# A decoder layer on one core: x's second half turned by VectorE, memory loaded earlier, GpSimd's units moved

## What is computed

```
h   = x + 1/2 * SwiGLU_1(norm(x))                 # w_ffn1_in, w_ffn1_out; d_ff = 5632
z   = norm(h) @ W_mix_in                          # columns B, C, H, U, V of 1024 each
y_c = B * causal_dwconv3(C * H)
y_g = U * (tril(W_s[head]) @ norm(V) + b)         # 8 heads x 128
h   = h + concat(y_c, y_g) @ W_mix_out
h   = h + XAttn(norm(h), norm(mem))               # 4 heads, w_xq, w_xk, w_xv, w_xo
h   = h + 1/2 * SwiGLU_2(norm(h))
out = norm_final(h)
```

## Time and profile before

| | |
|---|---|
| median of 3 runs (lowest to highest) | 2136.78 us (2136.63 to 2137.07) |
| the profiled execution: its time, its span | 2138.68 us, 2136.9 us |
| busy in the span: PE, DVE, ACT, POOL | 99%, 68%, 45%, 4% |
| traffic | 409 MB read, 192 GB/s over the span |
| share of the chain that ended last: PE, DVE, DMA | 95%, 3%, 1% |

### The profile page before, as it was taken

How to read it: one execution, slowest core, us unless ns; L and a number is a source line. 1 busy time by engine, 2 the same in 40 slices (tenths; PEclk the granted TensorE clock), 3 DMA queues, 4 the chain that set the end, 5 groups by cost and what they waited for, 6 DMA issues and landing times.

```text
span 2136.9 us, 23530 instructions
## 1 busy us (share of the span) xinstructions
PE 2124.8 (99%) x9480; PEld 1763.7 (83%) x9480; DVE 1462.7 (68%) x1754; ACT 964.2 (45%) x1090; POOL 92.9 (4%) x43
## 2 busy tenths in 40 slices
PE   9999999999999999999999999999999999999998
PEld 7888888888888888888888888888888888888887
...
GB/s 266 192 193 197 190 195 196 190 195 197 192 192 195 191 195 194 192 222 188 192 194 195 171 172 172 173 210 195 191 195 193 192 195 192 193 195 194 192 195 149
DMA packets 159825, 412.65 MB, mean 193 GB/s; under 512 B 12652, under 2 KB 14308, under 8 KB 159332
## 3 DMA queue, kind: packets, MB, share of 16 engines
...
HBM read 409.01 MB, written 2.10 MB: 192 GB/s over the span
## 4 chain that ended last, share of the span: by engine, by line
PE 95%; DVE 3%; DMA 1%; ACT 0%; issue 0%; ACTq 0%; DVEq 0%
PE ps L1180 94%; PE ps L1207 1%; DVE ps L745 1%; DVE w_lo L685 1%; DMA mem_nat<-in_mem 0%; DVE ps L1062 0%; PE ps L1265 0%; PE ps L1343 0%; DMA rows<-in_g_ffn 0%; PE ps L1230 0%; DVE memT_nat L756 0%; PE ps L1259 0%; DVE xT_lo L701 0%; DVE stage L848 0%; DVE stage L964 0%
## 5 line engine op out<-in xcount | busy, mean ns | idle before, releaser
L685 DVE TENSOR_TENSOR w_lo<-raw,w_hi 128x1024 fp32r<-128x1024 f32 x732 | 911.5, 1254 | 561.3 <-ACT w_hi L365 554.5
L365 ACT ACTIVATE w_hi<-raw 128x1024 fp32r<-128x1024 f32 x767 | 805.8, 1061 | 968.9 <-PE ps L1180 954.0
L1180 PE MATMUL ps<-w_hi,xT_hi 128*128 128x512 f32 x1848 | 494.5, 389 | 1.0 <-ACT w_hi L365 1.0
L1180 PE MATMUL ps<-w_lo,xT_hi 128*128 128x512 f32 x1848 | 493.9, 389 | 0.0
L1180 PE MATMUL ps<-w_hi,xT_lo 128*128 128x512 f32 x1848 | 493.9, 389 | 0.0
L1180 PEld LDWEIGHTS ps<-w_hi,xT_hi 128*128 128x128 f32 x1848 | 346.6, 188 | 73.3 <-DVE xT_lo L693 1.4
L1180 PEld LDWEIGHTS ps<-w_hi,xT_lo 128*128 128x128 f32 x1848 | 346.9, 188 | 72.0
L1180 PEld LDWEIGHTS ps<-w_lo,xT_hi 128*128 128x128 f32 x1848 | 346.9, 188 | 71.9
L745 DVE STREAM_TRANSPOSE ps<-stage 32x256 f32<-32x256 f32 (+1 forms) x464 | 241.4, 520 | 8.5
L1180 PE MATMUL ps<-w_hi,hidT_lo 128*128 128x512 f32 x700 | 188.5, 389 | 0.0
L1180 PE MATMUL ps<-w_lo,hidT_hi 128*128 128x512 f32 x700 | 188.5, 389 | 0.0
...
## 6 DMA issues: line engine op xcount, KB each, us to landing
...
```

The lines of the kernel that those rows point to most:

```text
L365: nc.scalar.activation(w_hi[:, u % RING, :], raw[:, u % RAW, :], ACT.Copy).then_inc(hi_ready, 1)
L685: nc.vector.tensor_tensor(w_lo[:, u % RAW, :], raw[:, u % RAW, :], w_hi[:, u % RING, :].bitcast(F32), ALU.subtract).then_inc(lo_ready, 1)
L1180: ins = nc.tensor.matmul(bank(s, t * GW + b * BLK, BLK), xs[:, k, t * P:(t + 1) * P], ws_[:, (unit0 + k) % (RING if ws_ is w_hi else RAW), ...
```

## The change

It has five parts.

1. x comes in six parts: tile 0 alone, tile 1 alone, then 2 and 3, 4 to 7, 8 to 11, 12 to 15. TensorE turns one identity block instead of four ahead of tile 0, tile 1 after the first passes of unit 0, tiles 2 and 3 a pass earlier.
2. Tiles 8 to 11 are turned by VectorE too, with the low parts of units 4 to 7 between the quarters; tiles 12 to 15 have those of units 9 to 12 between theirs. GpSimd makes the low parts of units 3, 5, 7, 9, 11 and 13 of this group instead of 7, 9, 11 and 13; such units are skipped in VectorE's list.
3. Memory is loaded in four parts of 512 KB inside V's weight loads, and SyncE's wait is gone. All of its first half is turned in U, the second in mix_out0 and mix_out1. `wsT`, which lay where memory goes, moves into `scratch`.
4. GpSimd's units in mix_out0 are now 5, 7, 9, 11, 13, 15 (they were the odd ones from 1), in k1 and v0 5, 7, 8, 10, 12, 14 (they were the odd ones from 5).
5. The gain product of the third piece of the end goes from VectorE to GpSimd.

The core of the diff:

```diff
-X_PARTS = ((0, 2), (2, 4), (4, 8), (8, 12), (12, 16))
+X_PARTS = ((0, 1), (1, 2), (2, 4), (4, 8), (8, 12), (12, 16))
...
-    pool_units = [*range(UNIT0["ffn1_in0"] + 7, UNIT0["ffn1_in0"] + 15, 2),
-                  *range(UNIT0["mix_out0"] + 1, done("mix_out1"), 2), *range(UNIT0["q0"] + 5, UNIT0["q0"] + 13, 2),
-                  *range(UNIT0["k1"] + 5, done("k1"), 2), *range(UNIT0["v0"] + 5, done("v0"), 2)]
+    pool_units = [*range(UNIT0["ffn1_in0"] + 3, UNIT0["ffn1_in0"] + 15, 2), *range(UNIT0["mix_out0"] + 5, done("mix_out0"), 2),
+                  *range(UNIT0["mix_out1"] + 1, done("mix_out1"), 2), *range(UNIT0["q0"] + 5, UNIT0["q0"] + 13, 2),
+                  *(UNIT0[name] + k for name in ("k1", "v0") for k in (5, 7, 8, 10, 12, 14))]
...
@@ SyncE @@
-            for name, c in (("C", 1), ("H", 2), ("B", 0), ("V", 4), ("U", 3)):
+            for name, c in (("C", 1), ("H", 2), ("B", 0)):
                 load_units(cols_src(w_mix_in, c * GW), UNIT0[name], KD)
-
-            sp.wait_ge(gated, 4)
-            sp.dma_start(mem_nat[:, :, :], mem[0].rearrange("(t p) n -> p t n", p=P)).then_inc(mem_loaded, 16)
+            for n in range(4):
+                load_units(cols_src(w_mix_in, 4 * GW), UNIT0["V"], 4 * n + 4, 4 * n)
+                t, c = n % 2, n // 2
+                sp.dma_start(mem_nat[:, t, c * GW:(c + 1) * GW], mem[0, t * P:(t + 1) * P, c * GW:(c + 1) * GW]
+                             ).then_inc(mem_loaded, 16)
+            load_units(cols_src(w_mix_in, 3 * GW), UNIT0["U"], KD)
...
@@ ScalarE @@
+            act.wait_ge(turned, TURN["x0"] + 1)
             nc.scalar.activation(xT_hi[:, 1, :], bank(1, 7 * SEQ, SEQ), ACT.Copy, scale=col("g_ffn1", 1)).then_inc(hi_taken, 1)
-            hi_units(0, 1, 2)
+            hi_units(0, 1, 3)
             hi_scaled(xT_hi, 0, "g_ffn1", 1, "x0", 1, 2)
-            hi_units(0, 2, 3)
             hi_units(0, 3, 4)
             hi_scaled(xT_hi, 0, "g_ffn1", 1, "x0", 2, 4)
-            hi_units(0, 4, 6)
+            hi_units(0, 4, 8)
             hi_scaled(xT_hi, HALF, "g_ffn1", 1, "x1", 0, 2)
-            hi_units(0, 6, 9)
+            hi_units(0, 8, 9)
...
@@ VectorE @@
-            lo_units(0, 4, 6)
-            lo_scaled(xT_lo, xT_hi, HALF, "g_ffn1", 1, "x1", 0, 2)
-            lo_units(0, 6, 7)
-            dve.wait_ge(x_loaded[4], 16)
-            dve.wait_ge(turned, TURN["x1"] + 2)
-            for q in range(4):
-                turn_blocks(h[:, :, 12 * P:D], 1, 4, 4 * q, 4 * q + 4, 4)
-                lo_units(0, 7 + q, 8 + q)
-            lo_units(0, 11, 12)
+            for part, u in ((4, 4), (5, 9)):
+                dve.wait_ge(x_loaded[part], 16)
+                for q in range(4):
+                    turn_blocks(h[:, :, X_PARTS[part][0] * P:X_PARTS[part][1] * P], 1, 4, 4 * q, 4 * q + 4, 4 * (part - 4))
+                    lo_units(0, u + q, u + q + 1)
+                if part == 4:
+                    lo_scaled(xT_lo, xT_hi, HALF, "g_ffn1", 1, "x1", 0, 2)
+                    lo_units(0, 8, 9)
             lo_scaled(xT_lo, xT_hi, HALF, "g_ffn1", 1, "x1", 2, 4)
-            lo_units(0, 12, 13)
...
-            lo_units(u, 8, 15)
-            dve.wait_ge(mem_loaded, 16)
-            turn_mem(0, u, 15, 0, 1)
-            turn_sbuf(memT_nat[:, 0:HALF, :], mem_nat[:, :, 0:GW], mem_turned, 2, 4)
+            lo_units(u, 8, 9)
+            dve.wait_ge(mem_loaded, 16 * 4)
+            turn_mem(0, u, 9, 0, 7)
+            turn_sbuf(memT_nat[:, 0:HALF, :], mem_nat[:, :, 0:GW], mem_turned, 14, 16)
...
-                lo_units(u, 3, 5)
+                lo_units(u, 3, 4)
                 dve.wait_ge(staged, STAGED[name] + TOK)
                 for i in range(4):
                     turn_blocks(stage[:, :, :], SET[name], HALF, 4 * i, 4 * i + 4)
-                    lo_units(u, 5 + i, 6 + i)
+                    lo_units(u, 4 + i, 5 + i)
...
-                lo_units(u, 9, 13)
+                lo_units(u, 8, 13)
...
-            end_gain(2)
             end_rstd(1, 4, 2)
...
@@ TensorE @@
-            group("ffn1_in0", xT_hi, xT_lo, 4, 5)
-            pe.wait_ge(x_loaded[3], 16)
+            group("ffn1_in0", xT_hi, xT_lo, 4, 6)
             pe.wait_ge(taken, TAKEN["x0"] + 4)
-            turn(from_half(h, 1), 1, 4, 0)
-            group("ffn1_in0", xT_hi, xT_lo, 5, 8)
+            group("ffn1_in0", xT_hi, xT_lo, 6, 8)
             pe.wait_ge(taken, TAKEN["x1"] + 2)
             group("ffn1_in0", xT_hi, xT_lo, 8, 12)
             pe.wait_ge(taken, TAKEN["x1"] + 4)
```

More of the change, by code:

```diff
@@ L135, in build @@
     stage = put("stage", [P, TOK, GW], F32)
+    at_scratch = place["at"]
     scratch = put("scratch", [P, GW], F32)
+    wsT = put("wsT", [P, HEADS, P], F32, at=at_scratch)
     ident = put("ident", [P, P], F32)
@@ L168, in build @@
     v_buf = put("v_buf", [P, TOK, GW], F32, at=big + 56 * KB)
-    wsT = put("wsT", [P, HEADS, P], F32, at=big + 64 * KB)
     sg = put("sg", [P, TOK, GW], F32, at=big + 80 * KB)
@@ L217, in build @@
         first_half = sem("first_half")
+        tile_turned = sem("tile_turned")
         tile_hi = sem("tile_hi")
@@ L253, in build @@
         gained = sem("gained")
+        gained_pool = sem("gained_pool")
         out_ready = [sem(f"out_ready{c}") for c in range(2)]
@@ L347, in low_units @@
                                             ALU.subtract).then_inc(lo_pool, 1)
-            low_units(pool_units[:4])
+            low_units(pool_units[:6])
             pool.wait_ge(ws_loaded, 16)
@@ L352, in _ @@
                                pattern=[[0, HEADS], [-1, P]], channel_multiplier=1).then_inc(ws_masked, 1)
-            low_units(pool_units[4:])
+            low_units(pool_units[6:])
+            pool.wait_ge(staged, STAGED["ffn2_out1"] + 3)
+            nc.gpsimd.tensor_tensor(stage[:, 1, 0:BLK], h[:, 1, GW:GW + BLK], g_fin[:, GW:GW + BLK],
+                                    ALU.mult).then_inc(gained_pool, 1)
         @block.scalar
@@ L455, in _ @@
             act.wait_ge(cols_ready, 1)
-            act.wait_ge(turned, TURN["x0"] + 1)
+            act.wait_ge(tile_turned, 1)
             nc.scalar.activation(xT_hi[:, 0, :], bank(1, 0, SEQ), ACT.Copy, scale=col("g_ffn1", 0)).then_inc(tile_hi, 1)
@@ L662, in _ @@
             nc.scalar.activation(h[:, 1, BLK:GW], h[:, 1, BLK:GW], ACT.Copy, scale=rstd[:, 1:2]).then_inc(end_ready[1], 1)
-            act.wait_ge(gained, TOK + 3)
+            act.wait_ge(gained_pool, 1)
             nc.scalar.activation(h[:, 1, GW:GW + BLK], stage[:, 1, 0:BLK], ACT.Copy,
@@ L973, in _ @@
             lo_plain(yT_lo, yT_hi, HALF + 4, SET["U"], 2, HI["U"] + 2, b0=2)
-            turn_mem(0, u, 11, 2, 7)
-            turn_sbuf(memT_nat[:, 0:HALF, :], mem_nat[:, :, 0:GW], mem_turned, 14, 16)
+            turn_mem(1, u, 11, 0, 4)
+            lo_units(u, 15, KD)
             u = UNIT0["mix_out1"]
@@ L984, in _ @@
                 lo_units(u, 4 + i, 5 + i)
-                if i < 5:
-                    turn_sbuf(memT_nat[:, HALF:KD, :], mem_nat[:, :, GW:D], mem_turned, 2 * i, 2 * i + 2)
+                if i % 2 == 0:
+                    turn_sbuf(memT_nat[:, HALF:KD, :], mem_nat[:, :, GW:D], mem_turned, 8 + i, 10 + i)
             lo_units(u, 12, 13)
@@ L1007, in _ @@
             norm("mix", halves, D, rstd[:, :])
-            turn_mem(1, u, 13, 5, 8)
+            lo_units(u, 13, KD)
             for c, running in enumerate(("q1", "k0")):
@@ L1274, in _, with turn_first @@
             nc.tensor.transpose(bank(0, 0, KD), rows[0:KD, :], ident[0:KD, 0:KD]).then_inc(rows_turned, 1)
-            warm(4)
-            pe.wait_ge(x_loaded[0], 16)
-            for k, at in ((0, 0), (1, 7 * SEQ)):
+            warm(1)
+            def turn_first(k, at):
+                pe.wait_ge(x_loaded[k], 16)
                 for t in range(TOK):
                     ins = nc.tensor.transpose(bank(1, at + t * P, P), h[:, t, k * P:(k + 1) * P], ident[:, :])
-            ins.then_inc(turned, 1)
+                return ins
+            turn_first(0, 0).then_inc(tile_turned, 1)
             warm(8)
@@ L1289, in _ @@
             first_pass(0, xT_lo, w_hi, (1,))
+            turn_first(1, 7 * SEQ).then_inc(turned, 1)
             pe.wait_ge(lo_ready, 1)
@@ L1294, in _ @@
             first_pass(1, xT_hi, w_hi, (0, 1))
+            pe.wait_ge(x_loaded[2], 16)
+            turn(from_half(h, 0), 1, X_PARTS[2][1], X_PARTS[2][0])
             pe.wait_ge(taken, TAKEN["x0"] + 1)
             first_pass(1, xT_lo, w_hi, (0, 1))
-            pe.wait_ge(x_loaded[1], 16)
-            turn(from_half(h, 0), 1, X_PARTS[1][1], X_PARTS[1][0])
             pe.wait_ge(lo_ready, 2)
```

11 lines of the change are left out of this document (6 added, 5 removed).

## The result

The changed kernel takes 2150.06 us (median of 4 runs, 2149.83 to 2151.25), the kernel before beside it 2136.93 (4 runs, 2136.63 to 2137.49): 13.1 us slower, a ratio of 1.0061 with a 95% interval from 1.0049 to 1.0073. The forecast was 2145.4 with a range up to 2148.5, so the direction is right and the size is not.

The account below looks back on a forecast made before the run. The prediction took TensorE to bound the kernel, so its every wait or transpose costs run time. Eight terms of gains and losses summed to +8.6 us on a span of 2136.9; it forecast 2145.4 us, range 2139.0 to 2148.5.

Parts of the forecast that it names:

- term 3: First group, unit 4: its low part waits behind VectorE's four transposes and GpSimd's unit 5; 2.3 us lost.
- term 5: First group, unit 12: its low part stands before xT_lo of tiles 12 to 15; 3.8 us lost.
- term 7: k1 and v0: unit 6's low part comes late behind GpSimd's unit 10; 3.6 us lost, bounds 0 and 4.
- term 6: Memory loaded earlier, in V: TensorE's wait for yT_lo in mix_out0 goes; 1.2 us won, worst case 0.
- term 8: The end: one gain product leaves VectorE's last chain for GpSimd; 0.15 us won.
- Term 1: The start, tile 0 first: 0.35 us won; between 1.1 won and 0.7 lost.
- T: Start of the eight transposes of tiles 4 to 7; 17.85 in the shown profile before, forecast 17.5.
- Terms 2 to 5: First group: 0.8 us won as eight transposes leave TensorE; 2.3, 1.4 and 3.8 lost at units 4, 8 and 9, 12.
- Term 4: First group, units 8 and 9: late operands from VectorE, ScalarE and GpSimd; 1.4 us lost, bounds 0.3 and 2.
- The clock rival: TensorE's clock falls after the rest in term 5, costing 1.3 us or twice that: 2146.7 to 2148; chance 0.05.

Follow-up runs that it names:

- e5: Kernel before with only the change's memory part (four-part load, transposes in U, mix_out0's GpSimd units, wsT): 2137.22 us, ratio 1.0001.
- e9: Kernel before, unaltered, run for another profiled execution: 2136.55 us.
- e10: Kernel before, unaltered, run for a third profiled execution: 2136.76 us.
- e13: Kernel before with GpSimd's units 1 and 3 of mix_out0 given to VectorE, memory still loaded late: 2137.68 us, ratio 1.0001.
- e1: The change with VectorE making xT_lo of tiles 12 to 15 ahead of unit 12's low part: 2147.9 us.
- e4: The change with the end undone, VectorE making the gain product again instead of GpSimd: 2149.4 us.
- e6: Kernel before with only the change's start (tile 0 apart, one warm transpose, tile 1 later): 2137.07 us, ratio 1.0000.
- e8: The change with VectorE making unit 4's low part ahead of its first four transposes of tiles 8 to 11: 2148.58 us.
- e11: The change, unaltered, run for another profiled execution: 2149.03 us.
- e12: The change with unit 10 of v0 given back to VectorE: 2147.3 us.
- e2: The change with TensorE running unread transposes during its waits in unit 4 and ahead of unit 12: 2147.24 us.
- e3: The change with GpSimd's units and VectorE's order in k1 and v0 put back as before: 2145.88 us.
- e7: Kernel before with both the change's start and its memory part: 2135.88 us, ratio 0.9993.

## Why the prediction was right and wrong

The direction and the waits were right, their sum was not. The step that failed first is that the sum counted each rest of TensorE that it forecast (2.3 us in term 3, 3.7 in term 5, 3.2 in term 7) as the rest alone and put the slow matmuls behind it at nothing: they cost some 1.5 us behind unit 12 and as much in v0. Beside it, term 6 counted a gain of 1.2 that two of three executions of the kernel before do not hold, and term 8 took 0.15 for won where 0.8 was lost. Term 1, too small by 1.1, hid a part of this.

- **Term 1, too small.** 0.35 us were forecast. Kernels with the old start (the shown one, e5, e9, e10, e13) have T from 17.26 to 18.70, median 17.85; those with the new one (the change, e1 to e4, e6 to e8, e11, e12) from 16.00 to 17.02, median 16.4: 1.45 us. Two steps failed. The prediction let only the waits for `yT_lo` and `w_hi` be won and left out the one for the row of gains: it is 0.61 to 0.72 us in all five executions with the old start and gone in all ten with the new, so the first matmul of unit 0 starts at 5.32 to 5.53 and not at 6.3. (That row lands 2.2 us after its issue instead of 2.9; that x's smaller first part makes room for it is likely, but no run tries it alone.) And in "if that moment stays, the eight matmuls of the first passes end at 9.1" the moment at which the clock rises does not stay: it differs from execution to execution, with either start, and those matmuls end near 7.3 in the change's shown execution and near 8.6 in e2's.
- **Terms 2 to 5.** That TensorE would wait in unit 4 (2.3 forecast, 2.11 measured) and ahead of unit 12 (3.7; 3.50), for these operands and by these orders, was right, and unit 12 at T + 33.0 (33.06) too. Term 4's 1.4 is there where the clock stayed up behind unit 4 (from unit 5 to unit 10 it is 15.11 us in e2, e4 and e11, for five units' 13.60: 1.5); where it fell, the slow matmuls fill that time. None of it counts by itself: e2 and e8 show that all ahead of unit 12 is free on TensorE's side, and only what lengthens VectorE's chain counts, as the prediction's own T + 33.0 has it. What is missing up to unit 16, 1.6 us (45.71 behind T for 44.1), is the low clock behind unit 12 (12.65 us for e2's 11.19), all but 0.1. That unit 16 came at 62.12, near the 61.6 that was to prove terms 1 to 5 together, is luck: T came 1.1 sooner than forecast and the clock took 1.5 back.
- **Term 6, wrong in its base.** "1.2 won" was read from an execution in which GpSimd came first. In e9 and e10 there is no wait to win, and e5 shows 0.0 in the medians. This is also most of the 1.9 us by which the shown profile lay above its median; the prediction carried that offset over as if it were outside the kernel.
- **Term 7, right in its wait.** GpSimd's unit 10 was forecast 18.27 us behind v0's unit 0 and came 18.26 behind it (1242.90 less 1224.64); the wait was 2.91 us for 3.2. e3 gives 4.97 in all for 3.6, above the term's bound of 4; the rest is again the clock, which fell there in the shown execution.
- **Term 8, wrong sign.** "0.15 won" took GpSimd's product for free, though term 3 rested on the same exclusion. It cost 0.8 (e4 0.78). The Trainium skill, SBUF — State Buffer, section on who interferes with whom, says that a VectorE instruction with two inputs in SBUF contends with a GpSimd instruction that reads SBUF. The row of 1.05 us agrees, for an instruction of one element per partition.
- **The clock rival, priced well and weighed badly.** It got 0.05 and one stretch of 1.3 to 2.6 us, where the terms forecast three rests. Behind unit 12 it came in all six profiles with a rest of 3.5 to 3.6 us and no other work for TensorE: units 12 to 16 take 12.65 to 13.83 us there, 11.19 in e2, so 1.5 to 2.6 each. The Trainium skill, TensorE: Matmul & The Clock Gate, section on HAM oscillation, says that long enough gaps in TensorE's work send the clock back. For the rests of 3.5 to 3.6 us the runs agree, six times of six; where rests of 2.1 and 2.9 us, shorter than the gaps that the page names, did the same in some executions, the runs decide. Such a stretch should have stood in the forecast itself, since term 5 forecast such a gap.

Against e9, whose span is 13.3 us shorter than the change's and near the medians' 13.1, the account closes: 7.54 up to unit 16 (54.58 and 62.12), nothing from there to v0's unit 0 (1217.11 and 1224.64), 5.0 in v0, 0.8 at the end. The forecast's +8.6 lacked 1.6 and 1.4 for the clock, 1.2 for term 6 and 0.95 for term 8, and had 1.1 too little gain in term 1: 12.65 in all, and e9's own start, 0.59 before the shown one's, makes 13.2.

Which parts of the change are worth keeping, e7 suggests: the start and the memory part together are the fastest kernel here, 1.4 us under the one before.
